# Memory keys of a hybrid decoder block: two 512-and-256-column products in place of three of 256, banks dealt anew, halves added before the split

## The reference

```python
def memory_cross_attention(qm, mem, mem_norm_g, w_mem_kv):
    kv = rms_norm(mem, mem_norm_g) @ w_mem_kv            # (256, 1024) @ (1024, 2048)
    km, vm = jnp.split(kv, 2, axis=-1)                   # 4 heads of 256 columns each
    s = jnp.einsum('bshd,bmhd->bhsm', qm * MEM_HEAD_DIM ** -0.5, km)
    p = jax.nn.softmax(s, axis=-1)
    return jnp.einsum('bhsm,bmhd->bshd', p, vm)
```

## Time and profile before

| what | value |
|---|---|
| median of 3 runs | 684.38 us (683.76 to 684.55) |
| the profiled execution | 683.92 us |
| its span in the profile | 682.1 us |
| granted TensorE clock, mean | 0.999 of 2.4 GHz |
| TensorE matmul busy | 673.5 us, 99% of the span |
| weight loads (beside them) | 616.4 us |
| VectorE, ScalarE busy | 493.5 us, 371.5 us |
| HBM traffic | 193 GB/s over the span |

### The profile page before, as it was taken

One profiled execution on the slowest core, in us unless ns is written; L12 is line 12 of the kernel. 1 busy time (PEld: TensorE's weight loads), 2 busy tenths in 40 slices (PEclk: granted clock), 3 DMA queues, 4 the chain that ended last, 5 costly groups with the idle time before them and its releaser, 6 DMA issues.

```text
span 682.1 us, 11417 instructions
## 1 busy us (share of the span) xinstructions
PE 673.5 (99%) x4505; PEld 616.4 (90%) x4505; DVE 493.5 (72%) x617; ACT 371.5 (54%) x462; POOL 10.4 (2%) x21
## 2 busy tenths in 40 slices
PE   8999999999999999999999999999999999999996
PEld 6999999999999989999888888888899999999995
DVE  6886979696866766777754655556688777777796
ACT  7568767767455544555533333443555555555552
POOL 0000000000100000000000000000100000000001
PEclk9999999999999999999999999999999999999999
DMA  9775868569185446545566655565445555555521
GB/s 297 240 256 181 247 198 263 164 217 326 62 270 171 145 163 232 180 140 171 178 211 218 214 194 182 195 231 173 166 140 191 188 185 190 180 189 183 193 87 62
DMA packets 99599, 130.92 MB, mean 192 GB/s; under 512 B 5615, under 2 KB 73708, under 8 KB 98924
## 3 DMA queue, kind: packets, MB, share of 16 engines
q1 hardware_dynamic: 98020, 125.27, 55.8%
q10 hardware_dynamic: 1544, 5.16, 2.3%
HBM read 129.31 MB, written 2.68 MB: 193 GB/s over the span
## 4 chain that ended last, share of the span: by engine, by line
PE 97%; DVE 1%; DMA 1%; ACT 0%; POOL 0%; issue 0%; POOLq 0%; SPq 0%; DVEq 0%; ACTq 0%
PE ps L364 31%; PE ps L365 30%; PE ps L366 30%; PE ps L678 1%; DMA x_nat<-x 1%; PE ps L679 1%; PE ps L419 1%; PE ps L663 1%; PE ps L698 1%; PE ps L715 1%; PE ps L706 0%; DVE h_nat L1750 0%; PE ps L697 0%; PE ps L717 0%; PE ps L771 0%; PE ps L666 0%
## 5 line engine op out<-in xcount | busy, mean ns | idle before, releaser
L336 DVE TENSOR_TENSOR w_lo<-w_raw,w_hi 128x2048 fp32r<-128x2048 f32 x107 | 244.6, 2287 | 88.0 <-ACT w_hi L332 88.0
L332 ACT ACTIVATE w_hi<-w_raw 128x2048 fp32r<-128x2048 f32 x107 | 204.3, 1911 | 99.1 <-PE ps L366 93.9
L364 PE MATMUL ps<-tok_hi,w_hi 128*128 128x256 f32 x864 | 246.6, 285 | 0.4 <-DVE tok_lo L1310 0.4
L365 PE MATMUL ps<-tok_lo,w_hi 128*128 128x256 f32 x864 | 244.4, 283 | 0.0
L366 PE MATMUL ps<-tok_hi,w_lo 128*128 128x256 f32 x864 | 244.4, 283 | 0.0
L364 PEld LDWEIGHTS ps<-tok_hi,w_hi 128*128 128x128 f32 x864 | 165.7, 192 | 2.0 <-issue 1.5
L365 PEld LDWEIGHTS ps<-tok_lo,w_hi 128*128 128x128 f32 x864 | 165.7, 192 | 0.4
L366 PEld LDWEIGHTS ps<-tok_hi,w_lo 128*128 128x128 f32 x864 | 165.7, 192 | 0.0
L364 PE MATMUL ps<-w_hi,tok_hi 128*128 128x512 f32 x128 | 50.2, 392 | 0.0
L365 PE MATMUL ps<-w_lo,tok_hi 128*128 128x512 f32 x128 | 49.9, 390 | 0.0
L366 PE MATMUL ps<-w_hi,tok_lo 128*128 128x512 f32 x128 | 49.8, 389 | 0.0
(11 more groups left out here) (269 smaller groups left out, 1002.2 us busy)
## 6 DMA issues: line engine op xcount, KB each, us to landing
w_raw<-w_in SPq DMA_DIRECT2D x94, 512.0 KB, 4.8
w_raw<-w_ffn_up SPq DMA_DIRECT2D x44, 512.0 KB, 4.4
w_raw<-w_ffn_down SPq DMA_DIRECT2D x22, 512.0 KB, 4.1
w_raw<-w_mem_kv SPq DMA_DIRECT2D x16, 512.0 KB, 4.4
w_raw<-w_br_ssm SPq DMA_DIRECT2D x16, 512.0 KB, 4.9
acs_b<-acs_d ACTq DMA_DIRECT2D x4, 1024.0 KB, 6.3
w_raw<-w_br_attn SPq DMA_DIRECT2D x8, 512.0 KB, 4.8
w_raw<-w_br_mem SPq DMA_DIRECT2D x8, 512.0 KB, 4.6
```

The source lines that it names most:

```text
L332: act.activation(w_hi[:, s, :], w_raw[:, s, :], ACT.Copy).then_inc(hi_ready[s], 1)
L336: dve.tensor_tensor(w_lo[:, s, :], w_raw[:, s, :], w_hi[:, s, :].bitcast(F32), ALU.subtract).then_inc(lo_ready[s], 1)
L364: pe.matmul(o, a[0], b[0], start=start, stop=False, **kw)
L365: pe.matmul(o, a[0], b[1], start=False, stop=False, **kw)
```

## The change

The key product is made by a new function. It keeps the weights' high part stationary for one matmul whose moving operand is the high and the low part of the tokens side by side (512 columns), then adds the weights' low part by the tokens' high part (256 columns) onto the first half. For that the tokens' parts are interleaved in one tile. The result lies in two halves, in banks 1 and 2 (one bank for each j): the first holds high by high and low by high, the second high by low. ScalarE copies the second half to SBUF, VectorE adds the first onto it, and high and low part of the key are then taken from the sum in SBUF. The values go to banks 3 and 5, the scores to bank 2, the attend step of self-attention pair 3 to bank 6. The first value product waits for the copies of the self-attention's probabilities (`pt_ready`, 8), and the wait for the attended tile moves from there to `attend(4)`. Three semaphores are merged into others.

```diff
+MK_BANKS, MV_BANKS = (1, 2), (3, 5)
-    tok_hi = place("tok_hi", 72, [KT, T], F32R)
-    tok_lo = place("tok_lo", 80, [KT, T], F32R)
+    tok = place("tok", 72, [KT, 2, T], F32R)
+    tok_hi, tok_lo = tok[:, :, 0, :], tok[:, :, 1, :]
-    me_hi = place("me_hi", R + 72, [KT, T], F32R)
-    me_lo = place("me_lo", R + 80, [KT, T], F32R)
+    me = place("me", R + 72, [KT, 2, T], F32R)
+    me_hi, me_lo = me[:, :, 0, :], me[:, :, 1, :]
+    km_sum = place("km_sum", 88.5, [2, T])
...
+    def gemm_both(pe, s, banks, both, other=None, tiles=None):
+        for j in range(2):
+            if other is not None and j:
+                pe.wait_ge(*other)
+            for k in range(KT):
+                if tiles is not None and j == 0:
+                    pe.wait_ge(tiles, k + 1)
+                w = slice(k * CW + j * P, k * CW + (j + 1) * P)
+                pe.matmul(ps[:, banks[j], :], w_hi[:, s, w], both[:, k], start=k == 0, stop=False)
+                mm = pe.matmul(ps[:, banks[j], 0:T], w_lo[:, s, w], both[:, k, 0, :], start=False, stop=k == KT - 1)
+        mm.then_inc(gemm_done[s], 1)
+    def part_pair(banks, n):
+        return ps[:, banks[0]:banks[1] + 1, n * T:(n + 1) * T]
...
-        return (7, 7, 2, 6)[n - 1]
+        return (7, 7, 6, 6)[n - 1]
...
             def mem_scores(i):
                 pe.wait_ge(qm_low, i + 1)
-                pe.wait_ge(bank_free[1], RC + 2 + i)
+                pe.wait_ge(km_low, i + 1)
...
-            gemm_cols(pe, RC, 1, me_hi, me_lo, tiles=(m_lo, 1))
-            pe.wait_ge(oa_lo_s, 3)
-            gemm_wide(pe, RC, 0, me_hi, me_lo)
+            def mem_keys(i):
+                pe.wait_ge(lo_ready[1], RC + i + 2)
+                pe.wait_ge(bank_free[1], RC + i + 1)
+                gemm_both(pe, 1, MK_BANKS, me, tiles=None if i else m_lo)
+            mem_keys(0)
+            pe.wait_ge(pt_ready, 8)
+            gemm_wide(pe, RC, 0, me_hi, me_lo, MV_BANKS)
             mem_scores(0)
             for i in range(1, 4):
                 gate1_part(i)
                 if i == 1:
+                    pe.wait_ge(oa_lo_s, 3)
                     attend(4)
                 else:
                     mem_attend(i - 1)
                 turn_mem_probs(i)
-                gemm_cols(pe, RC + i, 1, me_hi, me_lo)
-                gemm_wide(pe, RC + i, i % 2, me_hi, me_lo)
+                mem_keys(i)
+                gemm_wide(pe, RC + i, i % 2, me_hi, me_lo, MV_BANKS)
...
                 act.wait_ge(gemm_done[1], r + 1)
-                act.activation(km_hi[:], halves(1), ACT.Copy).then_inc(km_hi_s, 1)
+                act.activation(km_sum[:], part_pair(MK_BANKS, 1), ACT.Copy).then_inc(low_part, 1)
+                act.wait_ge(bank_free[1], r + 2)
+                act.activation(km_hi[:], km_sum[:], ACT.Copy).then_inc(km_hi_s, 1)
                 split_hi(act, r + 1, 1)
...
-                low(1, km_hi, km_lo, km_hi_s, i + 1, bank_free[1])
+                dve.wait_ge(low_part, 1 + i)
+                dve.tensor_tensor(km_sum[:], part_pair(MK_BANKS, 0), km_sum[:], ALU.add).then_inc(bank_free[1], 1)
+                dve.wait_ge(km_hi_s, i + 1)
+                dve.tensor_tensor(km_lo[:], km_sum[:], km_hi[:].bitcast(F32), ALU.subtract).then_inc(km_low, 1)
                 split_lo(dve, r + 1, 1)
...
-                    mm.then_inc(h_spread, 1)
+                    mm.then_inc(late_turned, 1)
...
-            dve.wait_ge(h_spread, 1)
+            dve.wait_ge(late_turned, 9)
```

More of the change, by code:

```diff
@@ L269, in build @@
         sem, ("group_mm", "group_var", "group_pow", "group_kept", "rstd_g_in"))
+    km_low, low_part = sem("km_low"), sem("low_part")
     s_mm, s_biased, s_max, s_neg, p_exp, p_rec, p_norm, p_turned, pt_ready, o_mm, oa_hi_s, oa_lo_s = map(
@@ L274, in build @@
     norm_step, os_hi_s, os_lo_s = map(sem, ("norm_step", "os_hi_s", "os_lo_s"))
-    m_in, m_sumsq, m_var, m_rstd, m_scaled, mx_in, m_factor_kept, m_factor_in, m_hi, m_lo = map(
-        sem, ("m_in", "m_sumsq", "m_var", "m_rstd", "m_scaled", "mx_in", "m_factor_kept", "m_factor_in", "m_hi", "m_lo"))
+    m_in, m_sumsq, m_var, m_rstd, m_scaled, mx_in, m_factor_moved, m_hi, m_lo = map(
+        sem, ("m_in", "m_sumsq", "m_var", "m_rstd", "m_scaled", "mx_in", "m_factor_moved", "m_hi", "m_lo"))
     ms_mm, ms_max, ms_neg, mp_exp, mp_rec, mp_norm, mp_turned, mo_mm, om_hi_s, om_lo_s = map(
@@ L286, in build @@
     out_done, h_added = sem("out_done"), sem("h_added")
-    h_sumsq, h_var, h_rstd, h_spread, rstd_b_ready, late_turned, h_hi, h_lo = map(
-        sem, ("h_sumsq", "h_var", "h_rstd", "h_spread", "rstd_b_ready", "late_turned", "h_hi", "h_lo"))
+    h_sumsq, h_var, h_rstd, rstd_b_ready, late_turned, h_hi, h_lo = map(
+        sem, ("h_sumsq", "h_var", "h_rstd", "rstd_b_ready", "late_turned", "h_hi", "h_lo"))
     pads_zero, conv_begun, f_step, g_tanh, g_silu, hid_done, hid_hi_s, hid_lo_s = map(
@@ L374, in wide_part, with gemm_wide @@
         return mm
-    def gemm_wide(pe, r, kh, hi, lo):
+    def gemm_wide(pe, r, kh, hi, lo, banks=V_BANKS):
         pe.wait_ge(lo_ready[2], r + 2)
@@ L381, in gemm_wide @@
         for t in range(NT):
-            mm = wide_part(pe, 2, t, kh, V_BANKS[t], hi, lo)
+            mm = wide_part(pe, 2, t, kh, banks[t], hi, lo)
         mm.then_inc(gemm_done[2], 1)
@@ L762, in mem_scores @@
                         cut = slice(t * P, (t + 1) * P)
-                        mm = three(pe, ps[:, 3, t * T:(t + 1) * T], (qm_hi[:, d, cut], qm_lo[:, d, cut]),
+                        mm = three(pe, ps[:, 2, t * T:(t + 1) * T], (qm_hi[:, d, cut], qm_lo[:, d, cut]),
                                    (km_hi[:, d, :], km_lo[:, d, :]), d == 0, d == 1)
@@ L1110, in _ @@
             act.wait_ge(m_rstd, NT)
-            act.dma_start(m_factor_d.rearrange("(p t) -> p t", p=P), stat[:, 2:2 + NT]).then_inc(m_factor_kept, 16)
+            act.dma_start(m_factor_d.rearrange("(p t) -> p t", p=P), stat[:, 2:2 + NT]).then_inc(m_factor_moved, 16)
             def mem_high(j):
@@ L1117, in _ @@
             squares(GROUPS)
-            act.wait_ge(m_factor_kept, 16)
-            act.dma_start(m_factor[:], on_all(m_factor_d, T)).then_inc(m_factor_in, 16)
+            act.wait_ge(m_factor_moved, 16)
+            act.dma_start(m_factor[:], on_all(m_factor_d, T)).then_inc(m_factor_moved, 16)
             for i in range(1, 4):
@@ L1175, in mem_head @@
                     for t in range(NT):
-                        act.activation(vm_hi[:, t, :], ps[:, V_BANKS[t], :], ACT.Copy).then_inc(vm_hi_s, 1)
+                        act.activation(vm_hi[:, t, :], ps[:, MV_BANKS[t], :], ACT.Copy).then_inc(vm_hi_s, 1)
                 act.wait_ge(ms_neg, i + 1)
                 for t in range(NT):
-                    act.activation(mprob[:, t, :], ps[:, 3, t * T:(t + 1) * T], ACT.Exp, bias=msoft[:, 1, t:t + 1],
+                    act.activation(mprob[:, t, :], ps[:, 2, t * T:(t + 1) * T], ACT.Exp, bias=msoft[:, 1, t:t + 1],
                                    scale=MDH ** -0.5, accum_out=msoft[:, 2, t:t + 1]).then_inc(mp_exp, 1)
@@ L1517, in heads @@
                 if i == 1:
-                    dve.wait_ge(m_factor_in, 16)
+                    dve.wait_ge(m_factor_moved, 32)
                     dve.wait_ge(mx_in, 16)
@@ L1580, in mem_head @@
                         dve.wait_ge(vm_hi_s, i // 2 * NT + t + 1)
-                        dve.tensor_tensor(vm_lo[t][:], ps[:, V_BANKS[t], :], vm_hi[:, t, :].bitcast(F32),
+                        dve.tensor_tensor(vm_lo[t][:], ps[:, MV_BANKS[t], :], vm_hi[:, t, :].bitcast(F32),
                                           ALU.subtract).then_inc(bank_free[2], 1)
                 dve.wait_ge(ms_mm, i + 1)
-                dve.tensor_reduce(msoft[:, 0, :], halves(3), AX, ALU.max).then_inc(ms_max, 1)
+                dve.tensor_reduce(msoft[:, 0, :], halves(2), AX, ALU.max).then_inc(ms_max, 1)
                 dve.wait_ge(ms_max, i + 1)
```

## The result

| | before | changed |
|---|---|---|
| median | 684.03 us (6 runs, 683.76 to 684.55) | 687.43 us (6 runs, 686.74 to 688.38) |
| ratio | | 1.0047, 95% interval 1.0036 to 1.0057 |
| the profiled execution | 683.92 us, span 682.1 | 688.38 us, span 686.6 |

A forecast was written before the change was run, and what follows sets the result against it. TensorE, busy 99% of the span, was taken to bound the kernel. Waits of 0.43 + 0.82 + 1.42 + 0.75 less 0.76 saved gave 2.66 us; 683.92 + 2.66 = 686.58, plus 0.46 to the median: 687.0, range 685.3 to 688.5.

The forecast's parts named there:

- What bounds: Whole kernel: TensorE busy 99% of the span; in the memory stage the ScalarE and VectorE chain is ready only just in time.
- Part 1, the product: Memory stage's key product: a pair takes 0.348 us in place of 0.359, saving 0.19 us a head, 0.75 in all.
- Part 2, the chain: ScalarE and VectorE after the key product: slot 1 split 1.37 us later; lateness 1.18, 1.83, 2.35, 2.87 in heads 0 to 3.
- the fourfold price: VectorE's add in the key chain: each 0.1 us reaches the last wait fourfold; sum 2.1 at 0.55, 3.7 at 0.96.
- Part 3, the first wait: First value product, now writing bank 3, waits 0.43 us for the last copies of the attention's probabilities.
- The waits at the turns and the last attend: Memory stage: TensorE waits 0.82 and 1.42 us at the turns of heads 1 and 3, 0.75 at the last attend.
- The cover: Rival, memory stage: the 1.37 us fits in the slack, no lateness builds up; 683.6, not slower; chance 0.10.
- the lateness did grow: Memory stage: lateness grows by half a microsecond a head, chance 0.75; rival, constant at 1.18, +1.0 to 685.4, chance 0.10.
- the granted clock: Rival: TensorE's clock falls after a 1.4 us wait; one merge product at 1.2 GHz adds 5.1, 692.1; chance 0.02.
- the product did not gain more: Rival, key product: gains over 21 ns an instruction and the cover holds, under 683.0; chance 0.03.

The follow-up runs named there:

- best_again: Second measurement of the changed kernel with gated norm before slot 1's low part, values to bank 5 first, attended tile and probabilities before slot 0's split: 683.52 us, before 684.20.
- norm_first: Changed kernel, but VectorE makes the four gated-norm multiplications before the low part of slot 1, not after it: 683.81 us, before 683.98.
- qlo_pool: Changed kernel, but the four subtractions for the low part of q move from VectorE to GpSimd: 686.13 us, before 683.86.
- v53: Changed kernel, but values go to bank 5 first, then 3, and the wait for the probabilities' copies stands before the first value product's second half: 686.87 us, before 683.98.

## Why the prediction was right, step by step

- **What bounds.** Right: TensorE at full pace, with a chain of ScalarE and VectorE that was ready only just in time.
- **Part 1, the product.** 0.347 us a pair in head 1. But 0.2 us were saved only in heads 1 and 2 (5.64 and 5.63 us in place of 5.83 and 5.84). In head 3 the product took 5.73, pairs of 0.353, and in best_again heads 0, 2 and 3 took 5.73 or 5.74. The saving of a version with no wait is therefore 0.5 and not 0.76; this term was sized half as large again as it measured. The code does not decide between the two paces: in the second execution of the changed kernel head 3 took 5.63. Head 1 is at 0.347 in all nine traces with the mixed product, head 0 at 0.353; head 2 is at 0.347 in the five whose turn before it waited and at 0.353 in the four whose turn did not. What selects the pace is open. The isolated gap of the Trainium skill (TensorE: Matmul & The Clock Gate, Back-to-back issue gap), whose constant of 2.5 ns a matmul makes 0.16 us in all, was too small for this trace: 0.49 us over 64 matmuls is 7.7 ns each. The prediction says that with the 2.5 ns its sum would be 0.6 us higher; by its own readiness of the last attend the saving enters only through head 0's lateness, so the sum would be 0.15 higher.
- **Part 2, the chain.** The add took 0.68 to 0.69, the copy from SBUF 0.63 (forecast 0.69 and 0.62), in the same operands that the rows bounded at 0.55 and 0.96. Lateness in head 0 was 1.30 and not 1.18, mostly because the first product saved 0.1 us and not 0.19 (the chain's first link itself was 1.41 longer and not 1.37); the steps after it were 0.65, 0.52 and 0.54, forecast 0.65, 0.52 and 0.52. norm_first and qlo_pool take away or reduce the growth and leave the first link at 1.3, as expected. No run shortens the first link alone, so the fourfold price that the prediction gives each 0.1 us of the add stays its arithmetic.
- **Part 3, the first wait.** The value product began 0.23 later than before, entry taken off (forecast 0.24). It is worth nothing in this kernel: v53 removed it and the stage's shift stayed 2.91. The prediction listed it as a term of 0.43 beside the others, though by its own figures the end is fixed by the last attend's readiness, 340.57 + 0.68 + 2.87 + 0.07, in which that wait does not occur. The total was right; read as separate prices the four waits and the saving mislead, since an earlier TensorE would only have waited longer at the next turn.
- **The waits at the turns and the last attend.** Listed at 0.65, 1.03 and 0.59. The list counts from the end of the preceding matmul's record, not from when the next could have started: TensorE's own starts move by 0.81, 1.19 and 0.75 there (shifts, entry off, 0.16 to 0.97, 0.84 to 2.03, 2.08 to 2.83), forecast 0.82, 1.42 and 0.75. The second is shorter because TensorE came to it 0.84 late and not 0.49.
- **The 0.26 us between 2.66 and 2.92.** The probabilities' low part, the operand of the last attend, was 3.01 late and not 2.87 (0.14, nearly all from head 0). The hand-over from VectorE to TensorE, put at 0.07 from no row, took 0.05 to 0.06 at the other waits and 0.10 here (0.03). After the wait the attend step itself took 0.09 longer, a term that the sum lacked; the same shows at the first value product, 5.58 us for 5.46. In the changed kernel's trace:

```profile
345.11 0.68 DVE L1564 TENSOR_TENSOR mprob_lo<-ps,mprob_hi 128x512 fp32r<-128x512 f32 x1
```

- **The rivals.** The cover did not hold; the lateness did grow; the granted clock stayed at 1.00 in the stretches 296 to 316 and 336 to 346 us, which hold the waits of up to a microsecond; the product did not gain more.
- **Whole run.** 2.92 in the stage; the medians differ by 3.4 in the first six runs and by 2.6 in the next five. That 687.0 lies only 0.4 from the measured 687.43 is in part luck: the median it started from was 0.35 higher than that of six runs, which made up for about half of a rise forecast 0.74 too small.

## What to carry to other kernels

Before lengthening a chain between two helper engines, add up the chain's period in a steady iteration, its waits included, and compare it with the bounding engine's. A helper that is idle for a quarter of the time can have no slack at all when its idle time is a wait inside the chain, and then whatever makes the chain's period longer than the bounding engine's is lost again in every iteration: here 1.3 us in the first head and half a microsecond in each one after. Such a loss can be one of order, as here: an independent instruction put into the helper's wait paid for the growth. And while the bounding engine waits for the chain at the end, next to nothing that it saves itself shows (here 0.08 us, where the mixed product itself was 0.6 shorter over the four heads).

## What was not expected of the hardware

- The pace of the mixed product has two values, 0.347 and 0.353 us a pair, each held as a mean through a whole product, and the same kernel had head 3 at either; no run here shows what selects it.
- GpSimd's subtraction of 128x512 took 1.33 us once and 2.90 us three times, and the VectorE instructions beside it were not longer (0.68 and 2.29). At the 1.33 VectorE was multiplying one tile by a column (L1542); at the 2.90 it was making the low part of slot 2 (L339, two operands from SBUF) for more than the first half. That this is the cause is not shown.
- A step that begins after a wait took about 0.1 us more than in an unbroken stream: the first value product 5.58 us for 5.46 (5.46 again in v53, which took the wait away), the last attend 0.09 more.
